# Two mixing layers of a transformer kernel: the up-projections as a split unit of the weight ring, the differential value products feature-major, one residual later

## The reference, cut to what is computed

```python
for l in range(2):
    h = rms_norm(x, attn_norm[l])
    proj = h @ w_in[l]                                  # [256, 2720]
    qa, ka, va, qb, kb, vb, qc, kc, vc, cq, ckv, kr = split(proj)
    o_a = neighborhood_attention(qa, ka, va, na_rpb[l])
    # differential attention, 4 heads: two score maps of 32 channels each
    a = softmax(s[0]) - lam * softmax(s[1])
    o_b = rms_norm(a @ vb, subln_g) * (1 - lam_init)    # norm over the 64 channels of a head
    o_c = dilated_attention(qc, kc, vc, t5_dil)
    # latent attention: ranks 256 (q) and 128 (kv), 4 heads
    qd = rms_norm(cq, mla_q_norm[l]) @ w_uq[l]          # [256, 4 * 96], rope on the last 32
    kvd = rms_norm(ckv, mla_kv_norm[l]) @ w_ukv[l]      # [256, 4 * 128], k_nope and v
    o_d = mla_attention(q_nope, q_rope, k_nope, apply_rope(kr), v_d)
    x = x + concat(o_a, o_b, o_c, o_d) @ w_o[l]
    h = rms_norm(x, ffn_norm[l])
    x = x + (silu(h @ w_gate[l]) * (h @ w_up[l])) @ w_down[l]
```

## Time and profile before

| | us |
|---|---|
| median of 3 runs | 1127.36 (1127.21 to 1127.59) |
| profiled execution, its own time | 1127.63 |
| profiled execution, span of its instructions | 1125.5 |
| PE busy | 1113.6 (99% of the span) |
| DVE busy | 782.1 (69%) |
| ACT busy | 535.3 (48%) |
| POOL busy | 108.7 (10%) |

### The profile page before, as it was taken

One profiled execution on the slowest core, in us unless ns is written; L12 is line 12 of the kernel. 1 busy time (PEld: TensorE's weight loads), 2 busy tenths in 40 slices (PEclk: granted clock), 3 DMA queues, 4 the chain that ended last, 5 costly groups with the idle time before them and its releaser, 6 DMA issues.

```text
span 1125.5 us, 16761 instructions
## 1 busy us (share of the span) xinstructions
PE 1113.6 (99%) x6437; PEld 967.4 (86%) x6437; DVE 782.1 (69%) x1020; ACT 535.3 (48%) x705; POOL 108.7 (10%) x200
## 2 busy tenths in 40 slices
PE   8999999999999999999999999999999999999997
PEld 7888888898888888888998888888899988888886
DVE  6876666767667666678686676676776866766675
ACT  5533333556654333346685533333456755333332
POOL 2000000000000000002860000000038400000000
PEclk9999999999999999999999999999999999999999
DMA  8865556664356555568953465556699444665550
GB/s 257 266 223 188 184 189 209 221 206 138 123 169 226 187 185 188 188 185 245 252 155 118 163 225 187 187 185 197 179 244 223 108 151 148 212 201 186 186 186 37
DMA packets 174151, 211.22 MB, mean 188 GB/s; under 512 B 22387, under 2 KB 157107, under 8 KB 174098
## 3 DMA queue, kind: packets, MB, share of 16 engines
q1 hardware_dynamic: 164322, 202.89, 57.1%
q0 software_dynamic: 9776, 7.62, 3.6%
HBM read 201.98 MB, written 1.16 MB: 180 GB/s over the span
## 4 chain that ended last, share of the span: by engine, by line
PE 96%; DVE 1%; ACT 1%; issue 1%; DMA 1%; POOL 0%; SPq 0%; DVEq 0%; POOLq 0%; ACTq 0%
PE bank L1615 26%; PE bank L1619 14%; PE bank L1589 13%; PE bank L1590 13%; PE bank L1591 13%; PE bank L1693 4%; PE bank L1901 2%; PE bank L1922 2%; PE bank L1628 1%; PE bank L1759 1%; PE bank L1654 1%; PE bank L1932 1%; PE bank L1685 1%; PE bank L2141 1%; PE bank L1631 1%
## 5 line engine op out<-in xcount | busy, mean ns | idle before, releaser
L680 ACT ACTIVATE whi<-raw 128x2048 fp32r<-128x2048 f32 x178 | 338.9, 1907 | 384.9 <-PE bank L1619 245.5
L1002 DVE TENSOR_TENSOR wlo<-raw,whi 128x2048 fp32r<-128x2048 f32 (+1 forms) x173 | 394.8, 2285 | 149.3 <-ACT whi L680 149.2
L1615 PE MATMUL bank<-h_both,whi 128*128 128x512 f32 x1280 | 304.6, 390 | 0.0
L1615 PEld LDWEIGHTS bank<-h_both,whi 128*128 128x128 f32 x1280 | 237.7, 188 | 47.8
L1589 PE MATMUL bank<-whi,o_hi 128*128 128x512 f32 x448 | 176.2, 393 | 0.0
L1590 PE MATMUL bank<-wlo,o_hi 128*128 128x512 f32 x448 | 174.9, 390 | 0.0
L1591 PE MATMUL bank<-whi,o_lo 128*128 128x512 f32 x448 | 174.4, 389 | 0.0
L1619 PEld LDWEIGHTS bank<-h_both,wlo 128*128 128x128 f32 x1280 | 164.1, 191 | 6.2
L1619 PE MATMUL bank<-h_both,wlo 128*128 128x256 f32 x1280 | 166.0, 283 | 0.0
L1591 PEld LDWEIGHTS bank<-whi,o_lo 128*128 128x128 f32 x448 | 84.1, 188 | 18.0
L1589 PEld LDWEIGHTS bank<-whi,o_hi 128*128 128x128 f32 x448 | 84.3, 188 | 17.6 <-issue 1.3
(11 more groups left out here) (202 smaller groups left out, 1319.8 us busy)
## 6 DMA issues: line engine op xcount, KB each, us to landing
raw<-in_w_gate_up SPq DMA_DIRECT2D x44, 1024.0 KB, 5.1
raw<-in_w_down SPq DMA_DIRECT2D x44, 1024.0 KB, 4.9
raw<-in_w_gate SPq DMA_DIRECT2D x22, 1024.0 KB, 5.4
raw<-in_w_up SPq DMA_DIRECT2D x22, 1024.0 KB, 5.3
raw<-in_w_in SPq DMA_DIRECT2D x18, 1024.0 KB, 8.1
raw<-in_w_o SPq DMA_DIRECT2D x12, 1024.0 KB, 5.0
raw<-in_w_kv SPq DMA_DIRECT2D x8, 1024.0 KB, 5.5
raw<-in_w_q SPq DMA_DIRECT2D x4, 1024.0 KB, 5.0
```

The costliest lines, as they stand in the source:

```text
L680: act.activation(whi[:, s, 0:w], raw[:, s, 0:w], ACT.Copy).then_inc(hi_ready, 1)
L1002: dve.tensor_tensor(wlo[:, s, 0:w], raw[:, s, 0:w], whi[:, s, 0:w].bitcast(F32), ALU.subtract).then_inc(lo_ready, 1)
L1615: pe.matmul(bank[bk + jj][:, :], hi[:, kc, jj * P:(jj + 1) * P], h_both[:, kc, :, :].rearrange("p a t -> p (a t)"), start=(kc == 0), stop= ...
```

## The change

- `w_uq` and `w_ukv` go through the ring as a unit of their own, ring number 4 of the layer (`UP_U`), 1536 columns wide. All later units of the layer move up by one (`ring`), and so do the unit numbers of what follows. The eight DMAs are now issued after unit 3 and ahead of unit 4; the k and v parts are gathered apart, in runs of 64 floats. ACT and DVE split the unit (`up`).
- The turned latents are held as `latT_hi` (ACT) and `latT_lo` (DVE, three new instructions), and `mla_G` uses `three`. k is made for two heads at once, 128 columns of weights.
- `split 4` moves behind `mla_T`, `split 5` behind `near_low 3` and ahead of `mla_G`, and ACT forms the residual of the first layer after `mla_G`. The DMAs of the biases that wait for that residual are issued two units later.
- Heads 8 to 11 go through `head_out`. ACT copies the result (`diff_copy`), PE turns it to tokens in bank 7 (`diff_turn`) between the two tiles of unit 10, and the norm goes on from there. `diff_T` turns back in bank 1, now behind unit 11, and the low half of the split of unit 12 moves behind the maxima of `S` 18 and 19.

```diff
-FFN_U = [1, 50, 98, 146]
+FFN_U = [1, 50, 99, 148]
-MIX_U = [83, 131]
+MIX_U = [83, 132]
+UP_U = 4
+UP_W = 1536
...
-    s += unit(2) + [("near_low", 2), ("mla_T",)] + unit(3) + [("near_low", 3), ("mla_G",)] + unit(4)
+    s += [("unit", 2), ("up",), ("proj", 2), ("near_low", 2), ("mla_T",), ("unit", 3), ("split", 4), ("proj", 3)]
+    s += [("near_low", 3), ("split", 5), ("mla_G",), ("residual",)] + unit(4)
...
-    s += TH(10, 11) + [("scores", 16), ("scores", 17)] + V(10, 11) + [("diff_stats",), ("exps", 16), ("exps", 17)] + N(16, 17) + [("diff_norm",)] + unit(10)
-    s += [("diff_T",)] + S(18, 19) + N(18, 19) + TH(12) + unit(11)
-    s += TH(13, 14) + V(12, 13) + TH(15) + unit(12)
+    s += TH(10, 11) + [("scores", 16), ("scores", 17)] + V(10, 11) + [("diff_copy",), ("exps", 16), ("exps", 17)] + N(16, 17)
+    s += [("tile", 10, 0), ("diff_turn",), ("tile", 10, 1), ("diff_stats",), ("high", 12), ("proj", 10), ("diff_norm",)]
+    s += S(18, 19) + TH(12) + [("low", 12)] + N(18, 19) + unit(11)
+    s += [("diff_T",)] + TH(13, 14) + V(12, 13) + TH(15) + unit(12)
...
             def load_layer(l):
-                if l:
-                    sp.wait_ge(mla_g, 3)
+                n = MIX_U[l] + UP_U
+                sp.wait_ge(lo_ready, n - 2)
+                wuq, wuk, wuv = up_weights(raw, l)
...
+                        dve.wait_ge(mla_tT, l + 1)
+                        for cc in range(3):
+                            e = dve.scalar_tensor_tensor(out=latT_lo[:, cc, :], in0=bank[cc // 2][:, (cc % 2) * T:(cc % 2 + 1) * T],
+                                                         scalar=mlag[:, l, cc:cc + 1], in1=latT_hi[:, cc, :].bitcast(F32),
+                                                         op0=ALU.mult, op1=ALU.subtract)
+                        e.then_inc(mla_tL, 1)
...
-                        pe.wait_ge(mla_tT, l + 1)
-                        pe.wait_ge(layer_in[l], 16 * 7)
+                        pe.wait_ge(mla_tL, l + 1)
+                        pe.wait_ge(lo_ready, u0 + UP_U + 1)
                         for h in range(4):
                             for kc in range(2):
-                                mm = pe.matmul(bank[h // 2][:, (h % 2) * T:(h % 2 + 1) * T], wuq[:, kc, h, :], latT[:, kc, :],
-                                               start=(kc == 0), stop=(kc == 1))
+                                mm = three(bank[h // 2][:, (h % 2) * T:(h % 2 + 1) * T], q_hi[:, kc, h, :], q_lo[:, kc, h, :],
+                                           latT_hi[:, kc, :], latT_lo[:, kc, :], kc == 0, kc == 1)
...
-                        if g == 2:
-                            pe.wait_ge(pt_ready, t_of[h] + 1)
-                            p = pt[:, (hd0 + h) % 4, :]
-                            for qt in range(2):
-                                for kt in range(2):
-                                    mm = pe.matmul(bank[6][:, qt * T + (h % 4) * HD:qt * T + (h % 4 + 1) * HD],
-                                                   p[:, kt * T + qt * P:kt * T + (qt + 1) * P],
-                                                   vg[:, par, kt, (h % 4) * HD:(h % 4 + 1) * HD], start=(kt == 0), stop=(kt == 1))
-                            mm.then_inc(pv_done, 1)
+                        head_out(hd0 + h, t_of[h], h % 4, [6, 7, 6, 0][g], vg[:, par], False)
...
+                    elif k == "diff_turn":
+                        pe.wait_ge(d_copied, l + 1)
+                        pe.wait_ge(out_lo, OUT_LO[l][1] + 1)
+                        for qt in range(2):
+                            for cc in range(2):
+                                mm = pe.transpose(bank[7][:, qt * T + cc * P:qt * T + (cc + 1) * P],
+                                                  dfm[:, cc * T + qt * P:cc * T + (qt + 1) * P], ident[:, :])
+                        mm.then_inc(d_turned, 1)
```

More of the change, by code:

```diff
@@ L370, in bass_two_stacks @@
                         freed[i0 + i] = q0 + nt + 1
-                if ev[0] in ("T", "diff_T"):
+                if ev[0] == "T":
                     nt += 1
@@ L386, in width_of, with ring, up_weights @@
         def width_of(n):
+            if n in (MIX_U[0] + UP_U, MIX_U[1] + UP_U):
+                return UP_W
             return LAT_K * LAT_W if n - MIX_U[0] in (0, 1) or n - MIX_U[1] in (0, 1) else UNIT
+        def ring(l, n):
+            return MIX_U[l] + n + (1 if n >= UP_U else 0)
+        def up_weights(w, l):
+            s = slot_of(MIX_U[l] + UP_U)
+            return (w[:, s, 0:1024].rearrange("p (k h n) -> p k h n", k=2, h=4), w[:, s, 1024:1280], w[:, s, 1280:UP_W])
         def slot_of(n):
@@ L554, in _ @@
                 for n in range(15):
-                    load(mix_src(l, n), MIX_U[l] + n)
-                    if n == 0:
+                    if n == UP_U:
                         load_layer(l)
+                    load(mix_src(l, n), ring(l, n))
                     if 1 <= n < 5:
@@ L563, in _ @@
                         load_na(l, n - 1)
-                    if n == 5 and l == 0:
+                    if n == 7 and l == 0:
                         sp.wait_ge(x_ready, 4 * 5)
@@ L901, in mix @@
                     k = ev[0]
-                    if k == "split":
-                        split(u0 + ev[1])
+                    if k in ("split", "high"):
+                        split(ring(l, ev[1]))
+                    elif k == "up":
+                        act.wait_ge(layer_in[l], 16 * 7)
+                        split(u0 + UP_U)
                     elif k == "proj":
@@ L935, in mix @@
                                                accum_out=msm[:, t, part:part + 1]).then_inc(mla_sq, 1)
+                    elif k == "mla_T":
+                        act.wait_ge(small_in, 15 * 16)
+                        act.wait_ge(mla_t, l + 1)
+                        for cc in range(3):
+                            e = act.activation(latT_hi[:, cc, :], bank[cc // 2][:, (cc % 2) * T:(cc % 2 + 1) * T], ACT.Copy,
+                                               scale=mlag[:, l, cc:cc + 1])
+                        e.then_inc(mla_tT, 1)
+                    elif k == "residual":
                         if l == 0:
@@ L941, in mix @@
                                     act.activation(x[:, t, cols], x_gained[:, t, cols], ACT.Copy, scale=rstd[:, t:t + 1]).then_inc(x_ready, 1)
[L942 to L948 removed]
                     elif k == "mla_G":
[L951 removed]
+                        act.wait_ge(mla_g, 2 * l + 1)
                         for c2 in range(2):
@@ L954, in mix @@
                                            ACT.Copy, scale=MLA_D ** -0.5)
-                        act.wait_ge(mla_g, 3 * l + 2)
-                        for c2 in range(2):
-                            act.activation(qall[0:HD, 4 + 2 * c2:6 + 2 * c2, :], bank[2 + c2][0:HD, :].rearrange("p (c k) -> p c k", c=2), ACT.Copy)
-                        act.wait_ge(mla_g, 3 * l + 3)
+                        act.wait_ge(mla_g, 2 * l + 2)
+                        for r in range(2):
+                            act.activation(qall[0:HD, 4 + r:8:2, :], bank[2][HD * r:HD * r + HD, :].rearrange("p (c k) -> p c k", c=2), ACT.Copy)
+                        act.wait_ge(units_used, u0 + UP_U + 1)
                         act.activation(vg[:, 0].rearrange("p a b -> p (a b)"), bank[6][:, :], ACT.Copy).then_inc(mla_copied, 1)
@@ L1475, in mix @@
                     k = ev[0]
-                    if k == "split" and ev[1] < 16:
-                        split(u0 + ev[1])
+                    if k in ("split", "low") and ev[1] < 16:
+                        split(ring(l, ev[1]))
+                    elif k == "up":
+                        split(u0 + UP_U)
                     elif k == "latent_out":
@@ L2035, in mix @@
                         n = ev[1]
-                        u = u0 + n
+                        u = ring(l, n)
                         bk = mix_bank(n)
@@ L2088, in mix @@
                         for t in range(TT):
-                            mm = pe.matmul(bank[6][:, t * T:(t + 1) * T], latT[:, 2, tile(t)], wukv[:, :, 1, :], start=True, stop=True)
-                        mm.then_inc(mla_g, 1)
+                            mm = three(bank[6][:, t * T:(t + 1) * T], latT_hi[:, 2, tile(t)], latT_lo[:, 2, tile(t)], v_hi, v_lo, True, True)
+                        used(mm)
                     elif k in ("S", "scores"):
```

86 lines of the change are left out of this document (43 added, 43 removed).

## The result

| | before | after |
|---|---|---|
| median, us | 1127.41 (1127.21 to 1127.59, 6 runs) | 1131.4 (1130.8 to 1132.41, 6 runs) |
| ratio to before, 95% interval | | 1.0036 [1.0025, 1.0047] |
| profiled execution, its own time | 1127.63 | 1132.41 |
| its span | 1125.5 | 1130.3 |

The change makes the kernel 0.36% slower, 4.0 us, where 5.4 us less were forecast. The granted PE clock over the whole span is 0.995, before 0.999.

A forecast was written before the change was run, and what follows sets the result against it. PE, busy 99% of the span, was taken as the bound. 6.75 us saved on PE less 1.4 us of waits gave 1127.36 - 5.35 = 1122.0 us, with a range of 1120.2 to 1125.8.

The forecast's parts named there:

- What bounds the kernel: Whole kernel: PE busy 99% of the span, so time off its chain, or a wait of it, counts whole.
- mla_G: PE, both mixing layers: 36 split matmuls 0.12 us apart replace plain float32 products, saving 2.06 us per layer.
- Value products: Heads 8 to 11 by head_out: 1.58 us saved less 0.72 us added, net 0.86 us per layer.
- The residual: First layer, ACT: moving it behind mla_G removes PE's wait of 0.91 us before unit 3.
- The norm of the differential heads: Behind diff_turn, before unit 11: its 4.0 us fit into 4.5 us of PE work; wait taken as 0.
- The sum: Time leaving PE over both layers: 2 x (2.06 + 0.86) + 0.91 = 6.75 us.
- Chain A: Up-projection load, splits and new DVE instructions into mla_G: ready at 531.9 us, PE wait 0 to 1.2 us.
- the two rivals on this load: Up-projections 2 to 3 us late per layer, 1124.6 to 1126.6 us (0.13); transfer meeting a full queue, 1132 us (0.06).
- the text's case of twice the time: k and v in 256 B runs taking some 3 us more, holding PE about 3 us per layer: 1126 us.
- Chain B: Load and split of unit 5, then rope, into the first scores: rope ends 543.2, PE wait 0 to 1.3 us.
- DVE 538.1: First layer: DVE's low half of the split of unit 5 takes 2.25 us and ends at 538.1.
- the load that meets a full queue: Up-projection load taking 15.7 us, PE waiting 11 us before mla_G in one layer: 1132 us, chance 0.06.

The follow-up runs named there:

- diff_only: Kernel before with only the differential part of the change (heads 8 to 11 by head_out, diff_copy, diff_turn, diff_T behind unit 11): 1125.31 us.
- mask_later: Changed kernel with POOL's mask moved behind all eight near copies, nothing left out: 1120.71 us, and 1121.27 us in a second comparison.
- mask_small: Changed kernel, order untouched, with POOL adding the neighborhood mask to only one column of each 64: 1121.08 us.
- fill: Changed kernel with 18 and 14 extra unused matmuls of 512 columns on PE ahead of the first scores in the two mixing layers: 1128.08 us.
- before_late_split: Kernel before with only the split of unit 5 moved behind near_low 3, ahead of mla_G: 1128.49 us, ratio 1.0008.
- before_mask_later: Kernel before with POOL's mask moved behind all eight near copies: 1127.49 us, ratio 0.9997.

## Why the prediction was wrong

**What bounds the kernel** was right: PE, whose every microsecond counts. It is also why the miss is so large.

**mla_G**, -2.06 us per layer: right. 36 matmuls 0.12 us apart from 531.89 to 536.21.

**Value products**, -0.86 us per layer net: right in mechanism, a little small. Two heads take 583.73 to 584.74, 1.01 us, so they pair. `diff_turn` takes 0.36 us and not 0.53, and the step back to split products is 0.08 us and not 0.19 (597.46 to 597.66 in place of 0.12). Between the value product of heads 6 and 7 and that of heads 14 and 15, diff_only takes 582.81 to 616.48, 33.67 us, and the kernel before 582.77 to 617.52, 34.75: 1.08 us per layer. The two layers give 2.2 us off the median, where 1.72 was said.

**The residual**, -0.91 us: right, a little small. PE starts unit 3 at 525.85 instead of 526.96, 1.1 us earlier, and the median falls by 1.2 to 1.35 us, depending on which median of the kernel before is taken (the interval allows 0.3 to 2.4). The idle time in a row of PE counts from the modelled end of the record before, and the next matmul can start ahead of that end: in the changed kernel unit 3 starts at 526.07, while the record of the transposes before it lasts to 526.31. The distance of starts is the price, and it is larger than the 0.91 of the row.

**The norm of the differential heads**, priced at nothing: right. PE has no wait there in the changed kernel.

**The sum**, 6.75 us: right as far as the runs can tell. In mask_later the first layer takes 506.69 to 625.29, 3.68 us less than before, and the second 809.74 to 927.31, 2.99 us less. Together 6.67 us, with 0.42 us of wait in them. The medians of its two comparisons lie 7.0 and 6.5 us below those of before, each with an interval of more than 1 us either way. The terms by themselves come to more, 4.12 + 2.2 + 1.2 = 7.5 us; `mla_G` never ran alone.

**Chain A** (0 to 1.2 us): no wait, but a close one in the first layer. The six DMAs of q were issued in 3.95 us, not 5.08, and landed after 2.4 to 3.3 us, not 4.7. This timeline of SP's queue shows the eight of them:

```profile
515.17 3.95 SPq L534 DMA_DIRECT2D raw<-in_w_uq  x6
519.17 0.63 SPq L536 DMA_DIRECT2D raw<-in_w_ukv  x1
519.84 0.63 SPq L537 DMA_DIRECT2D raw<-in_w_ukv  x1
```

The seventh, k, landed after 2.7 us. The eighth, v, took 5.3 us in the first layer (2.8 in the second) and was there at 525.1, where 525.6 was forecast; ACT sat idle for 2.80 us until then. That ACT was not later is the quicker issue and the slower landing together. ACT's split took 1.49 us and DVE's 1.76, DVE was through with its three new instructions at 531.63, and PE came at 531.89: 0.26 us to spare, and 1.1 us in the second layer. So the two rivals on this load didn't come, and the runs of 256 B cost PE nothing. Whether they are why the eighth took 5.3 us, or the 1 MB load issued 0.7 us behind it, no run shows. (By its own terms the text's case of twice the time comes to 1120.6 + 2 x 3 = 1126.6 us, not 1126.)

**Chain B** (0 to 1.3 us): this is the step that failed. Its order was right: load, ACT, DVE's low half, rope, scores. ACT was even through 0.2 us ahead of the 535.9 in the text. The failed term is "DVE 538.1", the low half at 2.25 us, taken from a row at 524.62 where POOL does nothing. The split was moved into a stretch in which POOL adds the mask, it took 6.10 and 6.48 us, and the rope ended at 546.16 instead of 543.2. With the terms of the text the wait was to be 1.3 us at most. It was 4.13 and 3.27.

A second term of the chain is wrong the other way, and for the same reason. The rope block of 5.12 us holds 0.86 us of POOL's mask already; in the changed kernel, behind the mask, it takes 541.89 to 546.16, 4.27 us. With 4.27 in its place and the split at 2.25 the text's terms give a wait of 0.4 us, and mask_small has 0.40.

The text asked of a moved instruction what it waits for and what is queued behind it, on DVE, ACT and SP. It didn't ask what runs beside it on POOL, and it read no row of POOL there. The kernel before had a sign of it: the rope's first addition, in the stretch that the earlier trace rows left out between 536.46 and 540.90, took 1.54 us and the second, identical one 0.68, the first beside POOL's mask and the second behind it. DVE and POOL in the kernel before:

```profile
537.89 1.54 DVE L1512 TENSOR_TENSOR qall<-pt 32x512 f32<-32x512 f32 x1
...
534.70 6.04 POOL L613 TENSOR_TENSOR bias<-bias,nmask 128x256 f32<-128x256 f32 x8
```

**The clock** had no term at all. A wait of PE was priced at its length. Of the 4.13 and 3.27 us the clock made 3.3 us more.

The waits account for the rest of the loss: 1121.0 (mask_later, the mean of its two medians) + 7.4 of waits less the 0.4 that it has itself = 1128.0, where fill stands at 1128.08. That it meets to 0.1 us is luck, since each of these medians is known to about 1 us. The 3.3 us of the clock are fill's distance to the changed kernel and so no second check. The mechanism for a slower kernel given in the text, the load that meets a full queue, is not the one that came.

## What to carry to other kernels

Price a moved instruction from a row in which the same neighbours run beside it, and look at every engine in the stretch into which it goes; for DVE with both inputs in SBUF that means POOL's rows first. Where two instances of one shape have different durations in the trace (1.54 and 0.68 us), find out why before moving anything near them. And where PE is the bound, a wait of several microseconds can cost more than its length (here 3.3 us on top of 7.4): look at the granted clock behind it.

## What the runs showed of the hardware

- An instruction of DVE with two SBUF inputs is held while POOL adds with both inputs in SBUF: 2.28 to 6.10, 6.48, 6.87 and 5.58 us (splits, 128 x 2048), 0.68 to 1.54, 3.69 and 4.57 us (32 x 512). With one input in PSUM (1.40 us for the two products of the rope) it isn't, nor beside POOL's short memsets, which only write (2.29 us).
- How long it is held varies. In the changed kernel DVE got no turn until all eight instructions were done; in the kernel before and in before_late_split it got one after the sixth; in mask_later, where DVE's split was running when the mask began, the rope's additions waited 0.41 us each, for one instruction of POOL. There POOL paid: 8.91 us for a mask of 5.66. In before_mask_later, where the mask began beside a product of the rope, the addition behind it was held for 3.9 us. What decides whose turn it is was not settled.
- Behind a wait of 4.1 us the granted clock was 0.50 from about 545 to 551.7 us, and behind one of 3.27 us it was 0.59 on average from 855 to 858. In fill, with PE at work, it stayed at 1.00. In mask_later, with a wait of 0.42 us, the clock over the span is 0.999.
